# A transformer block in one launch: inputs that arrive channel-major instead of being turned on the chip

## The chip, the cores and the metric

The kernel runs on one core of a Trainium2 chip. The metric is the device time of one execution in microseconds (us). The time before the change is 1368.11 us, the median of 3 runs (1367.45 to 1368.57). The engines are TensorE (PE in the rows; PEld is its weight load), VectorE (DVE), ScalarE (ACT), GpSimd (POOL) and SyncE (SP), whose queue issues all transfers. They run their own instruction lists in order and meet only at semaphores.

## The reference, cut to what matters

One block of a hybrid model, batch 1, 1024 positions, 1024 channels, 4 heads; all in float32. Only what the change touches is shown.

```python
def rmsnorm(x, g):
    xf = x.astype(F32)
    xf = xf * lax.rsqrt(jnp.mean(xf * xf, axis=-1, keepdims=True) + EPS)
    return (xf * g.astype(F32)).astype(x.dtype)

def causal_dwconv(x, w):            # 4 taps, per channel
    y = xp[:, 0:S] * w[0]
    for j in range(1, K):
        y = y + xp[:, j:j + S] * w[j]
    return y

def mlstm_mix(xn, w_in, conv_w, gate_b, norm_g, w_out):
    proj = xn @ w_in
    qk, v, o, g = jnp.split(proj, ...)
    qk = jax.nn.silu(causal_dwconv(qk, conv_w))
    ...                             # chunked scan over 64-step chunks, head norm, output product

memn = rmsnorm(mem, norm_mem)
h = x
h = h + mlstm_mix(rmsnorm(h, norm_mix), ...)
h = h + cross_attn(rmsnorm(h, norm_x), memn, w_q, w_kv, w_o)
h = h + swiglu(rmsnorm(h, norm_ffn), w_gate, w_up, w_down)
return rmsnorm(h, norm_final)
```

## The kernel before, in words

Every product is made of three TensorE products of a high and a low part (`WH`, `WL` of the weights, `XH`, `XL` of the activations); ACT makes the high part, DVE or POOL subtracts it from the full value to get the low one. Activations are kept with channels on the partitions: `xT` is 128 partitions x 8 channel tiles (k) x 1024 positions, worked on in two halves of 512. Weights come in strips of 1 MB into `raw`, in the order of the list `STRIPS`: the first value strip ("v", 0), then for each head its "qk", "v", "o" and the "wo" of the head before, then the memory keys "mk", the last "wo", the memory values "mv", and so on. A strip is worked in groups that go round four PSUM banks; a group can start when the group four before it was taken out of its bank. `PARTS` hangs pieces of other work (the scan of a head, a norm) in front of a group, in the same place on every engine.

**The start.** x arrives with positions on the partitions, in eight tiles of 128 positions x 1024 channels (4 KB a row): four into `xin` (in `VQ`), four into `xlate` (in `XT`). TensorE turns each with eight transposes (`turn_x`); DVE (`tile_of` copies) or ACT (`late_tile`) brings them to `xT`. ACT squares each tile along its row and sums it (`square_x`), POOL makes mean and power -0.5, TensorE spreads the result over the partitions (`spread`), and DVE multiplies x by it and by the gain (`norm`); ACT and DVE split that into `XH` and `XL` (`pieces`). The gain vectors and taps come as rows and are turned once into the columns `vcols`. `first_value(half)` is the value product of 4 position tiles, k by k, 12 products for each k: 4 with `XH` and `GW`, 4 with the weights' low part, 4 with `XL`. The late x tiles 5 to 7 are turned between its first k's. ACT empties the banks of the first half (`evac`) among its pieces of the second: it does the pieces (1, 0) and (1, 1) first, then group 3, whose bank the fourth tile of the second half needs (`bank_at`, `FIRST_OUT`).

**The memory norm.** Between the last "o" strip and the third "wo" strip (head 2) the memory, 256 positions, is normed: ACT squares its two tiles, POOL makes the factor `stat`, DVE multiplies tile, factor and gain (`memnorm`), TensorE turns the two tiles with 16 transposes in front of "wo" group 3 (`memturn`), ACT makes `MH` and DVE `ML` from the banks. The first part of the last head's scan stands in front of "wo" group 6, and waits on TensorE for all of `ML` (`s_ml`), as it uses the same banks.

**The convolution.** For each of the 16 "qk" groups DVE makes four passes over the bank into `acc`: a product with the last tap (L1687), then three multiply-adds (L1690), each linked to the one before; ACT then applies tanh.

Of the kernel before, what the change touches and what calls it, by code (L numbers as in the profile page):

```python
# [10 lines left out]
P = 128  # L11
# [5 lines left out]
def build_block(nc, x, mem, norm_mix, norm_x, norm_ffn, norm_mem, norm_final, a_w_in, a_conv_w, a_gate_b,  # L17
                a_norm, a_w_out, x_w_q, x_w_kv, x_w_o, f_w_gate, f_w_up, f_w_down, out):
# [142 lines left out]
    x_t = x[0].rearrange("(t p) d -> t p d", p=P)  # L161
    mem_t = mem[0].rearrange("(t p) d -> t p d", p=P)
    out_t = out[0].rearrange("(t p) d -> t p d", p=P)
# [8 lines left out]
    with ctx:  # L172
# [25 lines left out]
        NVEC = CONV + TAPS * KT  # L198
# [71 lines left out]
        mxs = mxin  # L270
        gain_mem, mjunk = xin[0], xin[1]
# [8 lines left out]
        vrows = QK[0:NVEC, 0, 0, 0:P]  # L280
# [118 lines left out]
        s_xt = sem("s_xt")  # L399
        s_xh = sem("s_xh")  # L400
        s_xl = sem("s_xl")
        s_vturn = sem("s_vturn")
# [15 lines left out]
        s_xta = sem("s_xta")  # L418
# [12 lines left out]
        s_wt = sem("s_wt")  # L431
        s_wi = sem("s_wi")
# [85 lines left out]
        def tile_of(t, unit):  # L518

            if t < 4 or t == TT - 1:  # L520
                k0, k1, b = 0, KT, 2 * t if t < 4 else 5
            else:
                k0, k1, b = 4 * unit, 4 * unit + 4, 5 + (2 * (t - 4) + unit) % 3
            src = PS[:, b:b + (k1 - k0) // 4, :].rearrange("p a s -> p (a s)").rearrange("p (k s) -> p k s", k=k1 - k0)
            return xT[:, k0:k1, t * P:(t + 1) * P], src

# [5 lines left out]
        def means(c):  # L532

            return 2 * (c + 1) if c < 2 else c + 3
# [55 lines left out]
        def _(sp):  # L590
            def load_strip(n):
# [11 lines left out]
            def load_mu(h):  # L603
# [3 lines left out]
                if h >= 2:  # L607
                    sp.wait_ge(s_wi, TT * (h - 1))
# [11 lines left out]
            for t in range(4):  # L620
                sp.wait_ge(s_xin[t], 16)
                sp.dma_start(xlate[t], x_t[4 + t]).then_inc(s_xin[t], 16)
                if t == 1:
                    sp.dma_start(dst[:, KT // 2:], src[:, KT // 2:]).then_inc(s_wdma, 16)
# [1912 lines left out]
```

## Time and profile before

| | |
|---|---|
| median of 3 runs | 1368.11 us |
| the profiled execution, its own time | 1368.82 us |
| its span in the profile | 1367.1 us |
| PE busy | 1353.3 us (99%) |
| DVE busy | 957.5 us (70%) |
| ACT busy | 511.6 us (37%) |
| POOL busy | 198.6 us (15%) |
| granted TensorE clock, mean | 0.999 |

The span is what the trace covers, the own time is the span with 1.7 us around it. A busy share says how full an engine is on average, not who waits for whom at a place: for that the trace is read by stretches.

### The profile page before, as it was taken

What the parts mean: (1) busy time and instruction counts of PE and PEld (TensorE: products, weight loads), DVE (VectorE), ACT (ScalarE), POOL (GpSimd) and SP (SyncE); (2) the same over time, 40 slices, a digit from 0 to 9 for tenths busy, and PEclk for the clock granted to TensorE, in tenths of its full rate; (3) what the DMA queues carried; (4) which work ended last, traced back from release to release, by engine and by line L of the source; (5) the groups of instructions that cost most, each with busy time, mean ns of one, the idle gap of its engine ahead of it and who ended that gap; (6) DMA issues with size and microseconds to landing.
All of it is one profiled execution on the core that took longest, in us unless ns stands there. A gap on an engine that the chain in (4) does not pass through costs nothing.

```text
span 1367.1 us, 18084 instructions
## 1 busy us (share of the span) xinstructions
PE 1353.3 (99%) x6795; PEld 1148.8 (84%) x6795; DVE 957.5 (70%) x1666; ACT 511.6 (37%) x910; POOL 198.6 (15%) x223
## 2 busy tenths in 40 slices
PE   8999999999999999999999999999999999999998
PEld 8889889889889988888888888888888888888886
DVE  7767467467488875454687966777778778877876
ACT  7323313313335553122345523444344435322224
POOL 3002202202203000000023000000000004544441
PEclk9999999999999999999999999999999999999999
DMA  5211111111223211010032233144434447989903
GB/s 187 62 62 55 55 31 50 60 31 44 97 71 126 85 60 47 17 62 32 31 129 103 78 116 116 55 154 162 169 138 148 154 163 267 329 282 318 341 31 124
DMA packets 110039, 158.56 MB, mean 116 GB/s; under 512 B 6560, under 2 KB 68096, under 8 KB 109952
## 3 DMA queue, kind: packets, MB, share of 16 engines
q1 hardware_dynamic: 109952, 157.39, 33.2%
q8 instruction: 55, 0.90, 0.3%
q14 instruction: 32, 0.26, 0.1%
HBM read 114.89 MB, written 42.48 MB: 115 GB/s over the span
## 4 chain that ended last, share of the span: by engine, by line
PE 90%; DVE 6%; issue 2%; ACT 2%; DMA 1%; POOL 0%; SPq 0%; DVEq 0%; POOLq 0%; ACTq 0%
PE PS L2076 14%; PE PS L2078 14%; PE PS L2077 14%; PE PS L2429 9%; PE PS L2428 9%; PE PS L2430 9%; PE PS L2460 5%; PE PS L2462 5%; PE PS L2461 5%; DVE WL L1757 1%; DVE acc L1690 1%; PE PS L2234 1%; PE PS L2236 1%; PE PS L2238 1%; PE PS L2141 1%
## 5 line engine op out<-in xcount | busy, mean ns | idle before, releaser
L2076 PE MATMUL PS<-XH,WH 128*128 128x512 f32 (+1 forms) x480 | 185.9, 387 | 0.0
L2078 PE MATMUL PS<-XH,WL 128*128 128x512 f32 (+1 forms) x480 | 180.3, 376 | 0.0
L2077 PE MATMUL PS<-XL,WH 128*128 128x512 f32 (+1 forms) x480 | 180.2, 375 | 0.0
L1674 DVE TENSOR_TENSOR xT<-PS,xT 128x512 f32<-128x512 f32 x128 | 87.5, 687 | 44.2 <-PE PS L2078 43.9
L2078 PEld LDWEIGHTS PS<-XH,WL 128*128 128x128 f32 x480 | 90.3, 188 | 16.7
L2076 PEld LDWEIGHTS PS<-XH,WH 128*128 128x128 f32 x480 | 90.4, 188 | 16.0 <-issue 0.4
L2077 PEld LDWEIGHTS PS<-XL,WH 128*128 128x128 f32 x480 | 90.5, 188 | 15.5
L2076 PE MATMUL PS<-YH,WH 128*128 128x512 f32 x256 | 101.4, 396 | 0.0
L2078 PE MATMUL PS<-YH,WL 128*128 128x512 f32 x256 | 99.8, 390 | 0.0
L2077 PE MATMUL PS<-YL,WH 128*128 128x512 f32 x256 | 99.7, 389 | 0.0
L1898 DVE TENSOR_TENSOR xT<-PS,xT 128x512 f32<-128x512 f32 x104 | 70.4, 688 | 39.6 <-PE PS L2462 38.5
L897 POOL TENSOR_TENSOR W2A<-raw,W2A 128x512 fp32r<-128x512 f32 x20 | 28.0, 1400 | 387.7 <-ACT W2A L1279 387.7
L2076 PE MATMUL PS<-WH,XH 128*128 128x256 f32 x256 | 74.2, 290 | 0.2 <-issue 0.2
L2078 PE MATMUL PS<-WH,XL 128*128 128x256 f32 x256 | 72.5, 283 | 0.0
L2077 PE MATMUL PS<-WL,XH 128*128 128x256 f32 x256 | 72.4, 283 | 0.0
L1835 DVE TENSOR_TENSOR U<-PS,U 128x512 f32<-128x512 f32 x50 | 33.5, 688 | 53.8 <-PE PS L2430 53.8
L1757 DVE TENSOR_TENSOR WL<-raw,WH 128x1024 fp32r<-128x1024 f32 x54 | 65.8, 1226 | 2.2 <-ACT WH L930 2.2
L2428 PE MATMUL PS<-XH,WA 128*128 128x512 f32 x160 | 62.2, 389 | 0.0
L2430 PE MATMUL PS<-XH,WA 128*128 128x512 f32 x160 | 62.2, 389 | 0.0
L2428 PE MATMUL PS<-XH,WB 128*128 128x512 f32 x160 | 62.2, 389 | 0.0
L2430 PE MATMUL PS<-XH,WB 128*128 128x512 f32 x160 | 62.2, 389 | 0.0
L1835 DVE TENSOR_TENSOR SG<-PS,SG 128x512 f32<-128x512 f32 x50 | 33.5, 686 | 34.3 <-PE PS L2430 32.7
(408 smaller groups left out, 3489.3 us busy)
## 6 DMA issues: line engine op xcount, KB each, us to landing
forms_hi<-HS SPq DMA_DIRECT2D x56, 256.0 KB, 2.3
raw<-in_f_w_up_dram SPq DMA_DIRECT2D x11, 1024.0 KB, 5.5
rawE<-in_f_w_gate_dram SPq DMA_DIRECT2D x10, 1024.0 KB, 5.7
raw<-in_f_w_down_dram SPq DMA_DIRECT2D x40, 256.0 KB, 4.0
forms_lo<-U SPq DMA_DIRECT2D x32, 256.0 KB, 2.3
XH<-forms_hi SPq DMA_DIRECT2D x16, 512.0 KB, 7.2
raw<-in_a_w_in_dram SPq DMA_DIRECT2D x7, 1024.0 KB, 5.0
XL<-forms_lo SPq DMA_DIRECT2D x12, 512.0 KB, 8.7
```

Of the source, the lines that this page charges most:

```text
L1674: v.tensor_tensor(xt, PS[:, g % NB, :], xt, ALU.add).then_inc(s_fd, 1)
L1757: last = v.tensor_tensor(WL[:, (n + 1) % 2, at], raw_of(n + 1)[:, at], WH[:, (n + 1) % 2, at].bitcast(F32), ALU.subtract)
L1898: v.tensor_tensor(x, bank_of(g, which), x, ALU.add).then_inc(s_ee, 1)
L2076: mm(dst, wh, xh, start=(k == 0), stop=False)
L2077: mm(dst, wh, xl, start=False, stop=False)
L2078: last = mm(dst, wl, xh, start=False, stop=(k == len(tiles) - 1))
L2428: mm(bank, w[:, i, 0, at], xh[:, kk, :], start=start, stop=False, skip_group_check=True)
L2429: mm(bank, w[:, i, 0, at], xl[:, kk, :], start=False, stop=False, skip_group_check=True)
L2430: last = mm(bank, w[:, i, 1, at], xh[:, kk, :], start=False, stop=stop, skip_group_check=True)
L2460: mm(bank, w[:, i, 0, at], xh[:, u, :], start=start, stop=False, skip_group_check=True)
L2461: mm(bank, w[:, i, 0, at], xl[:, u, :], start=False, stop=False, skip_group_check=True)
L2462: last = mm(bank, w[:, i, 1, at], xh[:, u, :], start=False, stop=stop, skip_group_check=True)
```

## The change

x, the memory and all norm gains and taps are also handed over channel-major (`x_turned`, `mem_turned`, `vec_cols`), made before the launch. At the start the first half of x goes straight into `xT` by four transfers of two channel tiles each; ACT squares the even k, DVE the odd k, and TensorE sums each square over the partitions with products against a column of ones (`square_sums`). The second half is loaded twice: by rows, for the squares on ACT, and channel-major for `xT`. All transposes of x, of the vectors and of the memory are gone. For the memory, the turned copy is loaded (`memT`), TensorE turns only the two factor columns, and DVE multiplies, k by k, memory, gain column and spread factor, in the place where `memturn` was; the work of DVE's `memnorm` is dropped. The convolution's first pass is done by ACT. The two semaphores of the scan's exponentials are merged into one. The diff, cut:

```diff
+        sqx = [VQ[:, k // 4, k % 4 * HALF:(k % 4 + 1) * HALF] for k in range(KT)]
+        memT = VQ[:, 0].rearrange("p (k m) -> p k m", k=KT)
+        mjunk = acc[:, :, :].rearrange("p a s -> p (a s)")
...
                 if n == AT["mk", 1]:
-                    sp.wait_ge(s_xs, MT)
-                    sp.wait_ge(s_sq, TT + MT)
+                    sp.wait_ge(s_ml, 2 * MT)
...
-            for t in range(4):
-                sp.dma_start(xin[t], x_t[t]).then_inc(s_xin[t], 16)
-            for v, at, n in ((norm_x, NORM_X, KT), (norm_ffn, NORM_F, KT), (a_norm, A_NORM, KT), (norm_mix, NORM_M, KT)):
-                sp.dma_start(vrows[at:at + n, :], v[0].rearrange("(k p) -> k p", p=P)).then_inc(s_vec, 16)
+            first = slice(0, HALF)
+            for i in range(4):
+                at = slice(2 * i, 2 * i + 2)
+                sp.dma_start(xT[:, at, first], x_k[:, at, first]).then_inc(s_xin[i], 16)
             dst, src = strip_src("v", 0)[0]
             sp.dma_start(dst[:, 0:KT // 2], src[:, 0:KT // 2]).then_inc(s_w0, 16)
             sp.dma_start(wg_raw, cols(a_w_in, G0, 2 * H)).then_inc(s_wg, 16)
+            sp.dma_start(vcols[:, :], vec_cols).then_inc(s_vec, 16)
+            sp.dma_start(dst[:, KT // 2:], src[:, KT // 2:]).then_inc(s_wdma, 16)
             for t in range(4):
                 sp.wait_ge(s_xin[t], 16)
                 sp.dma_start(xlate[t], x_t[4 + t]).then_inc(s_xin[t], 16)
+            for i in range(2):
+                at = slice(4 * i, 4 * i + 4)
+                sp.dma_start(xT[:, at, HALF:], x_k[:, at, HALF:]).then_inc(s_xlt, 16)
...
                     tap = CONV + KT * (TAPS - 1) + (r % 2) * H + h
+                    act.wait_ge(s_mm, g + 1)
+                    if c >= 2:
+                        act.wait_ge(s_qk, c - 1)
+                    sc.activation(acc[:, r % 2, :], bank, ACT.Copy, scale=vcols[:, tap:tap + 1]).then_inc(s_tap, 1)
                     act.wait_ge(s_conv, c + 1)
...
+            def square_chunk(i):
+                act.wait_ge(s_xin[i], 16)
+                sc.activation(sqx[2 * i], xT[:, 2 * i, 0:HALF], ACT.Square).then_inc(s_sq, 1)
...
             for k in range(KT):
                 pieces(0, (k,))
-                if k == 1:
-                    late_tile(4)
-                if k == 2:
-                    late_tile(5)
-                if k == 3:
-                    square_x(4)
-                    late_tile(6)
-                if k == 4:
-                    square_x(5)
-                if k == 5:
-                    square_x(6)
-                    square_x(7)
+                if 2 <= k <= 5:
+                    square_x(2 + k)
...
+            def memturn(a, b):
+                dve.wait_ge(s_gain, 16)
+                dve.wait_ge(s_turn, MT)
+                for k in range(KT):
+                    last = v.scalar_tensor_tensor(out=memT[:, k, :], in0=memT[:, k, :],
+                                                  scalar=vcols[:, NORM_MEM + k:NORM_MEM + k + 1], in1=X0[:, 0:M],
+                                                  op0=ALU.mult, op1=ALU.mult)
+                    if k % 4 == 3:
+                        last.then_inc(s_xs, 1)
+                for q in range(4):
+                    dve.wait_ge(s_mh, q + 1)
+                    at = slice(2 * q, 2 * q + 2)
+                    v.tensor_tensor(ML[:, at, :], memT[:, at, :], MH[:, at, :].bitcast(F32), ALU.subtract).then_inc(s_ml, 1)
...
                     if c == 1:
-                        dve.wait_ge(s_xta, 2 * NT - 2)
+                        dve.wait_ge(s_xlt, 32)
...
-                    if (c, k) in ((0, KT - 1), (1, KT - 1), (3, LATE[1]), (5, KT - 1)) and waiting:
+                    if (c, k) in ((1, KT - 1), (3, LATE[1]), (5, KT - 1)) and waiting:
                         make_lo()
...
-                    link(v.tensor_scalar(a, bank, tap(TAPS - 1), None, ALU.mult))
...
+            def keep_busy(count):
+                for _ in range(count):
+                    mm(PS[:, 7, 0:P], ones[:, :], ones[:, :], start=True, stop=True)
+
+            def square_sums(k):
+                pe.wait_ge((s_sq, s_sqv)[k % 2], k // 2 + 1)
+                for t in range(NT):
+                    last = mm(PS[:, t, 0:1], sqx[k][:, t * P:(t + 1) * P], one, start=(k == 0), stop=(k == KT - 1),
+                              skip_group_check=True)
+                if k == KT - 1:
+                    last.then_inc(s_xsum, 1)
...
-            for t in range(4):
-                turn_x(t)
+            for k in range(KT):
+                square_sums(k)
+            keep_busy(5)
             spread(0, 0)
+            keep_busy(5)
```

**TensorE at the start**, its first rows before (`ones` are products that only fill time, `VQ` holds the first four x tiles, `XT` the late ones, `small` the norm factor, `GW` and `WL` the first value weights):

```order
1 L2353 MATMUL PS<-ones 128x128 x7
2 L2347 MATMUL PS<-ident,VQ 128x128 x32
3 L2360 MATMUL PS<-ident,QK 128x64
4 L2363 MATMUL PS<-ident 128x128 x4
5 L2278 MATMUL PS<-ident,small 128x128 x4
6 L2347 MATMUL PS<-ident,XT_90 128x128 x8
7 L2163 MATMUL PS<-GW,XH 128x272 x4
8 L2168 MATMUL PS<-WL,XH 128x256 x4
9 L2172 MATMUL PS<-GW,XL 128x264 x4
10 L2347 MATMUL PS<-ident,XT_90 128x128 x8
```

and now (`VQ` holds the squares, `small` in row 2 is the column of ones):

```order
1 L2307 MATMUL PS<-ones 128x128 x9
2 L2313 MATMUL PS<-small,VQ 128x1 x32
3 L2307 MATMUL PS<-ones 128x128 x5
4 L2248 MATMUL PS<-ident,small 128x128 x4
5 L2307 MATMUL PS<-ones 128x128 x5
6 L2140 MATMUL PS<-GW,XH 128x272 x4
7 L2145 MATMUL PS<-WL,XH 128x256 x4
8 L2149 MATMUL PS<-GW,XL 128x264 x4
9 L2140 MATMUL PS<-GW,XH 128x272 x4
```

The 32 transposes have become 32 sums with one column each, 12 filling products are more (9, 5 and 5 for 7), and no transposes stand between the k's of the value product.

**VectorE at the end of the first half's norm**, before (a row with `s_rt` is the first norm of the second half; `XL` rows are low parts):

```order
16 L1587 SCALAR_TENSOR_TENSOR acc<-xT,vcols,PS 128x512 [waits s_xl]
17 L1733 COPY xT<-PS 128x8x128 [waits s_turn]
18 L1571 TENSOR_TENSOR XL<-SG,XH 128x512 [waits s_xh]
19 L1587 SCALAR_TENSOR_TENSOR acc<-xT,vcols,PS 128x512 [waits s_xl]
20 L1571 TENSOR_TENSOR XL<-acc,XH 128x512 [waits s_xh] x2
21 L1587 SCALAR_TENSOR_TENSOR SG<-xT,vcols,PS 128x512 [waits s_xl,s_xta,s_rt]
22 L1587 SCALAR_TENSOR_TENSOR SG<-xT,vcols,PS 128x512 [waits s_xl]
23 L1571 TENSOR_TENSOR XL<-SG,XH 128x512 [waits s_xh]
```

and now:

```order
19 L1576 SCALAR_TENSOR_TENSOR acc<-xT,vcols,PS 128x512 [waits s_xl]
20 L1560 TENSOR_TENSOR XL<-SG,XH 128x512 [waits s_xh]
21 L1576 SCALAR_TENSOR_TENSOR acc<-xT,vcols,PS 128x512 [waits s_xl]
22 L1560 TENSOR_TENSOR XL<-acc,XH 128x512 [waits s_xh]
23 L1576 SCALAR_TENSOR_TENSOR SG<-xT,vcols,PS 128x512 [waits s_xl,s_xlt,s_rt]
24 L1560 TENSOR_TENSOR XL<-acc,XH 128x512 [waits s_xh]
25 L1576 SCALAR_TENSOR_TENSOR SG<-xT,vcols,PS 128x512 [waits s_xl]
```

The copy of a turned tile is gone, and the low part of k = 7 of the first half (the second of row 20 before, row 24 now) has moved behind the first norm of the second half, which waits for its spread factor (`s_rt`) and its loads (`s_xlt`).

**VectorE at the memory norm**, around the third "wo" strip, before (`xT<-PS,xT` adds a "wo" group to the residual, `WL<-raw,WH` is the low part of the next weights):

```order
488 L1538 SCALAR_TENSOR_TENSOR QK<-QK,small,VQ 128x1024 [waits s_rs,s_gain]
489 L1538 SCALAR_TENSOR_TENSOR QK<-QK,small,VQ 128x1024 [waits s_rs]
490 L1532 TENSOR_SCALAR SG<-SG 128x512 [waits s_fa] x4
491 L1674 TENSOR_TENSOR xT<-PS,xT 128x512 [waits s_mm]
492 L1757 TENSOR_TENSOR WL<-raw,WH 128x1024 [waits s_whi]
493 L1674 TENSOR_TENSOR xT<-PS,xT 128x512 [waits s_mm]
494 L1757 TENSOR_TENSOR WL<-raw,WH 128x1024 [waits s_whi]
495 L1674 TENSOR_TENSOR xT<-PS,xT 128x512 [waits s_mm]
496 L1546 TENSOR_TENSOR XL<-PS,XH 128x4x128 [waits s_mh] x4
497 L1674 TENSOR_TENSOR xT<-PS,xT 128x512 [waits s_mm] x3
```

and now:

```order
475 L1521 TENSOR_SCALAR SG<-SG 128x512 [waits s_fa] x4
476 L1663 TENSOR_TENSOR xT<-PS,xT 128x512 [waits s_mm]
477 L1736 TENSOR_TENSOR WL<-raw,WH 128x1024 [waits s_whi]
478 L1663 TENSOR_TENSOR xT<-PS,xT 128x512 [waits s_mm]
479 L1736 TENSOR_TENSOR WL<-raw,WH 128x1024 [waits s_whi]
480 L1663 TENSOR_TENSOR xT<-PS,xT 128x512 [waits s_mm]
481 L1528 SCALAR_TENSOR_TENSOR VQ<-VQ,vcols,PS 128x256 [waits s_turn,s_gain]
482 L1528 SCALAR_TENSOR_TENSOR VQ<-VQ,vcols,PS 128x256 x7
483 L1536 TENSOR_TENSOR XL<-VQ,XH 128x512 [waits s_mh] x4
484 L1663 TENSOR_TENSOR xT<-PS,xT 128x512 [waits s_mm] x3
```

Two multiplications of 1024 elements ahead of the strip have become eight of 256 inside it, directly in front of the four low parts that complete `s_ml`.

## Rows read from the trace of the kernel before

**Rows 1.** Busy time by stretch: us, PE, PEld, DVE, ACT, POOL, clock, DMA.

```profile
42.00:130.00 88.00, 87.74 (x448) 74.11 (x447) 61.72 (x159) 28.17 (x59) 6.17 (x10) 1.00 0.19 58
```

**Rows 2.** PE's waits over the span: us in total, times, longest.

```profile
PE PS L2201 <- DVE hs L1505: 0.8, 3, 0.3
```

**Rows 3.** The start in order of time: start us, us, what.

```profile
4.44 1.06 ACT L935 ACTIVATE QK<-VQ 128x1024 f32<-128x1024 f32 x1 [2.36 <-DMA VQ<-in_x_dram]
9.36 1.09 PE L2347 MATMUL PS<-ident,VQ 128*128 128x128 f32 x8 [0.18 <-DMA VQ<-in_x_dram]
11.44 0.65 PE L2278 MATMUL PS<-ident,small 128*128 128x128 f32 x4 [0.20 <-POOL small L850]
12.13 1.41 DVE L1587 SCALAR_TENSOR_TENSOR SG<-xT,vcols,PS 128x512 f32<-128x512 f32 x2
13.69 0.74 PE L2163 MATMUL PS<-GW,XH 128*128 128x272 f32 x4
```

**Rows 4.** One line's instructions: count, ns min/median/max, first and last start.

```profile
L2353 PE MATMUL PS<-ones x14: 421/421/579, 1.2 to 4.1; 128*128 128x128 f32 x14
```

**Rows 5.** The column sums of the next norm, and POOL's power, in order of time.

```profile
450.01 1.05 PE L2262 MATMUL PS<-small,QK 128*128 128x1 f32 x8 [0.26 <-DVE QK L1556]
451.10 0.16 DVE L1563 COPY small<-PS 128x4 f32<-128x4 f32 x1 [0.55 <-PE PS L2262]
451.63 1.02 POOL L860 TENSOR_TENSOR small<-small 128x4 f32<-128x4 f32 x1
```

**Rows 6.** The first value product in order of time.

```profile
23.12 1.06 ACT L935 ACTIVATE QK<-XT 128x1024 f32<-128x1024 f32 x1
29.41 0.53 PE L2163 MATMUL PS<-GW,XH 128*128 128x272 f32 x3
30.12 0.39 PE L2163 MATMUL PS<-GW,XH 128*128 128x272 f32 x1 [0.18 <-ACT zg L1108]
```

**Rows 7.** The chain that ended last, inside the second half.

```profile
32.94 0.50 PE PS L2163 x4
...
34.41 0.51 PE PS L2163 x4
```

**Rows 8.** DMA activity at the start, columns as in rows 1.

```profile
16.00:17.00 1.00, 1.00 (x11) 1.00 (x10) 1.00 (x3) 0.70 (x2) 0.90 (x1) 1.00 0.26 85
```

**Rows 9.** The memory norm in order of time.

```profile
374.67 1.91 ACT L930 ACTIVATE WH<-raw 128x2048 fp32r<-128x2048 f32 x1
...
376.95 1.21 DVE L1757 TENSOR_TENSOR WL<-raw,WH 128x1024 fp32r<-128x1024 f32 x1
378.07 1.91 PE L2247 MATMUL PS<-ident,QK 128*128 128x128 f32 x16
...
380.42 2.47 DVE L1546 TENSOR_TENSOR XL<-PS,XH 128x512 fp32r<-128x512 f32 x4
...
383.91 0.27 PE L2218 MATMUL PS<-ident,QK 128*128 128x128 f32 x1
```

**Rows 10.** TensorE in the same stretch: where "wo" group 3 begins.

```profile
379.73 0.48 PE L2076 MATMUL PS<-YH,WH 128*128 128x512 f32 x1
```

**Rows 11.** Two DVE instructions in a row: 256 elements from PSUM, then another.

```profile
389.52 0.48 DVE L1501 TENSOR_SCALAR hs<-PS,small 128x256 f32<-128x256 f32 x1
389.92 0.68 DVE L1674 TENSOR_TENSOR xT<-PS,xT 128x512 f32<-128x512 f32 x1
```

**Rows 12.** The same multiplication form as the new one, 257 elements, by line.

```profile
L1491 DVE SCALAR_TENSOR_TENSOR Cst<-Cst,decay,PS x24: 474/482/485, 105.1 to 423.2; 128x257 f32<-128x257 f32 x24
```

**Rows 13.** After the last matmul, columns as in rows 1; the clock stands third from the end.

```profile
1360.00:1361.00 1.00, 0.29 (x2) 0.00 (x0) 0.67 (x2) 0.00 (x0) 0.53 (x1) 1.00 0.67 274
...
1363.00:1364.00 1.00, 0.00 (x0) 0.00 (x0) 0.86 (x2) 0.00 (x0) 0.10 (x1) 0.96 0.95 393
1364.00:1365.00 1.00, 0.00 (x0) 0.00 (x0) 0.55 (x1) 0.00 (x0) 0.00 (x0) 0.50 0.57 227
```

**Rows 14.** The convolution's first and later passes, by line.

```profile
L1687 DVE TENSOR_SCALAR acc<-PS,vcols x16: 740/745/751, 47.2 to 321.6; 128x512 f32<-128x512 f32 x16
```

More of the change, by code:

```diff
@@ L993, in memturn @@
                 act.wait_ge(s_mm, used(AT["o", H - 1]))
[L994 to L999 removed]
+                for q in range(4):
+                    act.wait_ge(s_xs, q // 2 + 1)
+                    at = slice(2 * q, 2 * q + 2)
+                    sc.activation(MH[:, at, :], memT[:, at, :], ACT.Copy).then_inc(s_mh, 1)
             def square(n, r):
@@ L1145, in split_first @@
                               ACT.Copy).then_inc(s_w0h, 1)
-            for t in range(4):
-                square_x(t)
+            for i in range(4):
+                square_chunk(i)
             split_first()
@@ L1711, in evac @@
                     add_residual(g, r)
-            for t in range(4):
-                dve.wait_ge(s_turn, t + 1)
-                dst, src = tile_of(t, 0)
-                v.tensor_copy(dst, src).then_inc(s_xt, 1)
-            dve.wait_ge(s_vturn, 1)
-            link(v.tensor_copy(vcols[:, :], PS[:, 0, 0:NVEC]))
+            for i in range(4):
+                dve.wait_ge(s_xin[i], 16)
+                full = xT[:, 2 * i + 1, 0:HALF]
+                v.tensor_tensor(sqx[2 * i + 1], full, full, ALU.mult).then_inc(s_sqv, 1)
+            dve.wait_ge(s_xsum, 1)
+            sums = PS[:, 0:NT, 0:1].rearrange("p t a -> p (t a)")
+            v.tensor_scalar(nmean[:, 0, :], sums, 1.0 / D, EPS, ALU.mult, ALU.add).then_inc(s_nm, 1)
+            dve.wait_ge(s_vec, 16)
             dve.wait_ge(s_wgs, 1)
@@ L1726, in _ @@
                             ALU.subtract).then_inc(s_wlo, 1)
-            norm(0, 5)
-            make_lo()
-            waiting.append((0, 5))
-            norm(0, 6)
-            dve.wait_ge(s_turn, TT)
-            dst, src = tile_of(TT - 1, None)
-            v.tensor_copy(dst, src).then_inc(s_xt, 1)
-            make_lo()
-            waiting.append((0, 6))
-            pieces(0, (7,))
+            pieces(0, range(5, KT))
             pieces(1, range(KT))
@@ L2241, in memturn @@
             def memturn(a, b):
+                pe.wait_ge(s_rs, MT)
+                pe.wait_ge(s_yf, TT * (H - 1))
                 for t in range(MT):
-                    pe.wait_ge(s_xs, t + 1)
-                    if t == 0:
-                        pe.wait_ge(s_yf, TT * (H - 1))
-                    for q in range(KT):
-                        last = nc.tensor.transpose(PS[:, NB + 2 * t + q // 4, (q % 4) * P:(q % 4 + 1) * P],
-                                                   mxs[:, t, q * P:(q + 1) * P], ident[:, :])
-                    last.then_inc(s_turn, 1)
+                    nc.tensor.transpose(X0[:, t * P:(t + 1) * P], stat[:, t, 2:3].to_broadcast([P, P]),
+                                        ident[:, :]).then_inc(s_turn, 1)
             def sumsq(which, half):
@@ L2351, in _ @@
+            def square_sums(k):
[5 more added lines that the diff above has]
+                    last.then_inc(s_xsum, 1)
             pe.wait_ge(s_const, 2)
-            for _ in range(7):
-                mm(PS[:, 7, 0:P], ones[:, :], ones[:, :], start=True, stop=True)
+            keep_busy(9)
```

145 lines of the change are left out of this document (46 added, 99 removed).

## The prediction, made before the changed kernel ran

> **What bounds the kernel now.** I read the busy time by stretch first: from 42 us on TensorE is busy 87.74 of 88 us [rows 1], and the later stretches look alike. Then its waits: the longest behind the start is 0.8 us in three pieces, for the scan's `hs` [rows 2]. So a microsecond taken from VectorE or ScalarE in the middle is worth nothing, and one taken from TensorE is worth one, as long as it doesn't come to wait. Only two places matter: the start, where TensorE waits for x, the norm and the splits, and the memory norm, where 16 transposes are in its list. I read both in order of time.
>
> **The start, up to the first norm.** Before: the first x tile is there at 4.44, the last is turned from 9.36, the spread starts at 11.44, the first norm at 12.13, the first value product at 13.69, 1.56 behind it [rows 3]. Now the same 2 MB come first, so I let them land at the same times (4.4 to 9.3). The nine filling products are 18 entries in the trace where seven were 14; those began between 1.2 and 4.1, 0.223 apart [rows 4], so 18 reach to about 5.1 (a little less if the later ones run faster). The first square (half of the 1.06 us of a 1024-wide one, so about 0.6 [rows 3]) is ready by then. Then come 32 column sums. The nearest row is exact in form: four of them are 8 entries and take 1.05 us, the last being visible 0.15 behind its place, so 0.11 each and 0.89 for four [rows 5]. Eight k's make 7.1 us: from 5.1 to 12.3. They are spaced so that TensorE, not the landing at 9.3, sets the end (the last two k's alone would need 1.8 from about 10.0). Then, as after the later sums: 0.1 to VectorE, 0.2 there, 0.1 to POOL, 1.02 for a power of four columns [rows 5], 0.06 to TensorE and 0.65 for the spread [rows 3], 0.04 to VectorE: first norm at 14.5. The five filling products in between (10 entries at 0.11) lie inside POOL's 1.3 us, the other five inside the 1.56 us from norm to product. **So the first norm comes 2.4 us later.** Bounds: if a column sum cost only its one column, the end would be set by the last landing, 9.3 + 0.65 + some 0.2, plus 2.2 of chain, 12.3: +0.2. If all ran at the spacing of the first fillers, 0.223, the sums would take 14.3 us: +9.6.
>
> The Trainium skill, page "TensorE: Matmul & The Clock Gate", section "Back-to-back issue gap", gives about 60 cycles for a matmul of 1 to 64 columns, some 25 ns. By that rule 64 entries would be an estimated 1.6 us, the sums would hide behind the landing, and the whole sum below would be 2.2 us less. The row is of the same instruction with its weight load and decides.
>
> **From the first norm to the second half.** Before, the second half's first product starts at 29.41 [rows 6], 17.28 behind the first norm. In that time TensorE also turned three late tiles, VectorE copied one, ScalarE copied three. Without them I lay the lists out anew, t from the first norm: a norm on VectorE 0.67 (two in 1.41 [rows 3]), a low part 0.60 (four in 2.47 [rows 9]), a weights' low part 1.2 [rows 9], on ScalarE a high part 0.6 and a late square 1.06 [rows 6], on TensorE 1.47 a k (32.94 to 34.41 [rows 7]). k = 0 starts at 1.56; k = 4 needs the second half of the weights' low part, behind the norm of k = 4 on VectorE: 7.7 instead of 7.4; the low part of k = 4 is then 0.3 late; k = 5 at 9.5, k = 6 at 10.95. At 12.4 stands the second spread (0.45); its power is ready at about 11.5. The low part of k = 7 now stands behind the first norm of the second half, which waits for that spread: norm 13.05 to 13.7, low part to 14.4, wanted at 13.85: 0.6 of stall. The second half starts at 14.95: **2.3 us gained**. One wait grows: its fourth tile needs the bank that ScalarE empties behind pieces (1, 0) and (1, 1). The norm of (1, 1) now ends at 15.1, ScalarE's piece at 15.75, the emptying at 16.4, against 15.35 wanted (three products of 0.13 [rows 7] behind the start): 1.05 of stall, where before it was 0.33 (30.12 against 29.41 and the same three [rows 6]): **0.7 lost**. The transfers: before, all was landed just after 16 us [rows 8]; x's second copy adds 2.1 MB, and at the pace of x's tiles, three of 0.52 MB from 4.44 to 9.3 [rows 3], that is 6.5 us, to 23; the norm of the second half wants it at 27.5. Hidden by 4.5 us; without the cover it would cost what it is late. Start in all: 2.4 - 2.3 + 0.7 = **+0.8 us**.
>
> **The convolution.** 16 passes of 0.745 [rows 14] leave VectorE, 12 us, and some 16 of 0.6 come to ScalarE, which waits there for the passes anyway. TensorE is four banks ahead; it gets at most the 0.8 us of rows 2 from it. I take -0.2, bounds -0.8 and, if ScalarE comes late with a first pass because of the scan in its list, +0.5.
>
> **The memory norm.** Before: the 16 transposes start at 378.07 [rows 9], "wo" group 3 at 379.73 [rows 10], the scan's first part behind group 5 at 383.91 [rows 9]: 1.66 for the transposes, 4.18 for three groups. VectorE is done with `ML` at 382.89 (380.42 + 2.47 [rows 9]), 1.0 before it is wanted. Now the two transposes leave group 3 at 378.3 and the scan's part comes up at 382.45. But VectorE: the strip's weights are ready at 376.6 (374.67 + 1.91 [rows 9]), its two low parts and two residual adds take 3.5 as before (376.95 to 380.42 [rows 9]), from 376.65 since `memnorm` is out of the way: 380.1. Then eight multiplications of 256 elements with a PSUM operand: of that form one lasts 0.48 [rows 12], and 0.40 passes from one such to the next instruction [rows 11]: 3.2. Then four low parts, 2.5 with the last one's end: 385.8. ScalarE's four high parts keep ahead (its last at 384.6). So `s_ml` is complete at 385.8 instead of 382.9, TensorE stands for 3.4 us and the scan's part starts at 385.85: **+1.9 us** against 383.91. Bounds: no wait left, -1.45 (14 transposes); multiplications at their full 0.48, +2.6. Nothing later gives it back, since TensorE is the bound; VectorE has evacuations of groups 3 to 5 behind it (to 387.8), and the bank of group 3 is free at 386.5, before group 7 wants it. The transfer of the next key weights now waits for `s_ml` as well, 10 us later than before; it lands by 392 and nobody reads it before the memory keys, past 400.
>
> **The sum.** 0.8 - 0.2 + 1.9 = +2.5 us. The profiled execution took 1368.82 (span 1367.1 and 1.7 around it), so it would take 1371.3; it lies 0.7 over the median of the runs shown, so the median goes from 1368.11 to **1370.6**, 0.18% slower. 0.2% (2.7 us) is about what a measurement of this kernel can tell from no change, so this lies just inside.
>
> **The rivals.**
> *The clock falls during the sums, slower.* For 7 us TensorE would do nothing but load weights and send one column. The first fillers took 421 ns each, with the column of the granted clock at 1.00 [rows 4]; a product of the same size lasts 270 later [rows 9], so these ran at the lower level of 1.2 GHz, and behind some 3.3 us of fillers back to back it was over. After the last matmul the granted clock falls to 0.50, 3.6 us later (0.96 in the mean of 1363 to 1364) [rows 13]. If it falls during the sums, say for their second half, those run at 0.22 apart (+3.9), the next fillers outlast POOL (+0.9), the spread and the first products are slow (+1.7): 6.5 more, 1377. No row shows TensorE at such work for longer than 1 us, so little speaks for or against. The same could strike the 3.4 us stall at the memory norm, which is just short of 3.6. Chance 0.2. The skill, in the same page's section "What's actually happening", says that the slow state is the default and activity releases it, which bears on this rival; by it the time would be the same 1377.
> *VectorE keeps up at the memory norm.* If the chain from 380.1 ends before 382.45, the transposes are a pure gain: 0.8 - 0.2 - 1.45, 1367.3. It needs multiplications and low parts in 2.3 us where rows give 5.7; only if TensorE comes there late for another reason. Chance 0.12.
> *The sums hide, not slower.* If a column sum costs what its column does, the first norm is at 12.3, and the whole -2.2 + 2.5: 1368.4. It decides from 0.05 us an entry down, where the landing at 9.3 takes over. Chance 0.12; together with the one before, 1365.1, another 0.08: the only clear gain.
> The forecast itself 0.48, spread from 1369 to 1372.
>
> **The numbers.** Faster by over 0.2% is below 1365.4: the double case and a little, 0.12. Slower by over 0.2% is above 1370.8: the clock's 0.2 and 0.46 of the forecast's 0.48, 0.42. Within: 0.46. For the range I leave out the double gain below and the dear end of the clock's case above: 1366.5 to 1376.5; the forecast's own is 1369 to 1372.
>
> **What will show it.** The first norm at 14.5, the 64 sum entries from 5.1 to 12.3, 0.11 apart; the second half's first product at 29.4 or 29.5 with a wait for ScalarE's `zg` of 1 us behind it; all later work shifted by 0.8. At the memory norm a wait of TensorE for `XL` from VectorE of 3.4 us, the largest behind the start, in front of the scan's transposes. It is wrong if the sums' spacing is not 0.11, if the granted clock or the durations show the lower level beyond 5 us, or if TensorE doesn't wait for `XL`.

## The result, and the profile after

The changed kernel took **1377.56 us** in the median of six runs (1376.48 to 1378.87), the kernel before 1367.87 (1367.32 to 1368.57, six runs beside them): ratio 1.007, 95% interval 1.006 to 1.008. It is 9.7 us slower, where 2.5 were forecast, and outside the range. The profiled execution spans 1375.1 us, 8.0 more than before.

The changed kernel in order of time, first the start, then the memory norm (start us, us, what):

```profile
4.86 0.63 ACT L1131 ACTIVATE VQ<-xT 128x512 f32<-128x512 f32 x1 [2.79 <-DMA xT<-in_x_turned_dram]
5.63 11.38 PE L2313 MATMUL PS<-small,VQ 128*128 128x1 f32 x64 [0.43 <-ACT VQ L1131]
9.15 0.63 ACT L1131 ACTIVATE VQ<-xT 128x512 f32<-128x512 f32 x1 [0.69 <-DMA xT<-in_x_turned_dram]
16.88 2.48 PE L2307 MATMUL PS<-ones 128*128 128x128 f32 x10
17.30 1.04 POOL L842 TENSOR_TENSOR small<-small 128x4 f32<-128x4 f32 x1 [14.44 <-DVE small L1705]
19.15 1.06 PE L2248 MATMUL PS<-ident,small 128*128 128x128 f32 x4
20.25 1.41 DVE L1576 SCALAR_TENSOR_TENSOR SG<-xT,vcols,PS 128x512 f32<-128x512 f32 x2 [2.88 <-PE PS L2248]
21.96 0.75 PE L2140 MATMUL PS<-GW,XH 128*128 128x272 f32 x4
...
384.56 3.21 DVE L1528 SCALAR_TENSOR_TENSOR VQ<-VQ,vcols,PS 128x256 f32<-128x256 f32 x8
387.69 2.49 DVE L1536 TENSOR_TENSOR XL<-VQ,XH 128x512 fp32r<-128x512 f32 x4
390.32 0.30 PE L2195 MATMUL PS<-ident,QK 128*128 128x128 f32 x1 [3.32 <-DVE XL L1536]
395.02 0.27 PE L2195 MATMUL PS<-ident,QK 128*128 128x128 f32 x1
```

These answer to [rows 3] and [rows 9]. The transfers land nearly as forecast (4.86 to 9.15, against 4.4 to 9.3). The 64 entries of the column sums last 11.38 us in place of 7.1, although TensorE does nothing else; the first norm stands at 20.25 (forecast 14.5, before 12.13) and the first value product at 21.96. The same kernel by stretch (us, PE, PEld, DVE, ACT, POOL, granted clock, DMA), which answers to [rows 1] and [rows 13]:

```profile
6.00:8.00 2.00, 2.00 (x20) 2.00 (x20) 0.86 (x2) 0.80 (x2) 0.00 (x0) 1.00 1.02 362
8.00:10.00 2.00, 2.00 (x12) 2.00 (x13) 1.22 (x2) 1.09 (x2) 0.00 (x0) 0.57 1.12 348
10.00:20.00 10.00, 10.00 (x47) 10.00 (x48) 0.31 (x2) 1.20 (x2) 2.70 (x3) 0.50 1.06 403
20.00:22.00 2.00, 2.00 (x12) 2.00 (x11) 1.71 (x3) 0.94 (x2) 1.77 (x2) 0.52 0.93 353
22.00:24.00 2.00, 2.00 (x18) 2.00 (x18) 2.00 (x4) 1.24 (x3) 0.00 (x0) 1.00 0.06 18
42.00:130.00 88.00, 88.00 (x456) 74.92 (x455) 57.46 (x151) 32.65 (x66) 3.89 (x7) 1.00 0.20 61
386.00:390.00 4.00, 1.00 (x5) 0.50 (x3) 4.00 (x9) 2.88 (x6) 0.00 (x0) 1.00 0.00 0
390.00:391.00 1.00, 0.68 (x4) 0.71 (x5) 1.00 (x3) 0.34 (x2) 0.00 (x0) 0.78 0.00 0
391.00:394.00 3.00, 3.00 (x8) 2.33 (x8) 2.08 (x6) 0.61 (x3) 0.00 (x0) 0.50 0.80 249
394.00:400.00 6.00, 6.00 (x29) 4.99 (x29) 4.20 (x12) 1.46 (x5) 0.73 (x2) 1.00 0.64 225
```

The granted clock, third from the end, falls to 0.50 during the sums (near 8.3 us, by the mean of 0.57 over 8 to 10) and is back when the value products run; twenty entries show in the two microseconds before the fall, 47 in the ten behind it. It falls once more behind the stall at the memory norm, for some 3.4 us. That stall heads TensorE's waits (us in total, times, longest); the wait of [rows 2] for `hs` is gone:

```profile
PE PS L2195 <- DVE XL L1536: 3.3, 1, 3.3
PE PS L2307 <- POOL small L781: 1.2, 1, 1.2
PE PS L2178 <- DVE yf L1505: 0.6, 2, 0.4
```

**Where the 8.0 us lie.** I cut the two traces at four places that both have. The first 512-wide product starts at 47.47 instead of 41.58: start +5.9. From there to the transposes of the memory norm 335.05 us instead of 336.49: middle -1.4. From those to the scan's first part 7.80 instead of 5.84: +2.0. From there to its second part 4.70 instead of 3.12: +1.6. From there to the end nothing. The places that no row above shows, before and then changed:

```profile
41.58 0.39 PE L2076 MATMUL PS<-XH,WH 128*128 128x512 f32 x1
...
387.03 0.27 PE L2218 MATMUL PS<-ident,QK 128*128 128x128 f32 x1
```

```profile
47.47 0.39 PE L2055 MATMUL PS<-XH,WH 128*128 128x512 f32 x1
...
382.52 0.38 PE L2222 MATMUL PS<-ident,small 128*128 128x128 f32 x2
```

### The profile page after: what moved, and what is told of

Its sections match the earlier page's. It is cut to its first block, busy times and chain, and to the rows that moved or that the text cites. A ratio compares the mean times of both kernels' runs of the same rounds, so it can differ in the third digit from the quotient of the medians.

```text
span 1375.1 us, 18072 instructions
## 1 busy us (share of the span) xinstructions
PE 1360.0 (99%) x6800; PEld 1157.5 (84%) x6800; DVE 943.0 (69%) x1655; ACT 517.1 (38%) x916; POOL 195.3 (14%) x220
## 4 chain that ended last, share of the span: by engine, by line
PE 66%; DVE 3%; issue 1%; ACT 1%; POOL 0%; DVEq 0%; POOLq 0%; ACTq 0%
PE PS L2389 9%; PE PS L2388 9%; PE PS L2387 9%; PE PS L2055 7%; PE PS L2057 7%; PE PS L2056 7%; PE PS L2419 5%; PE PS L2420 5%; PE PS L2421 5%; DVE WL L1736 1%; PE PS L2120 1%; PE PS L2122 1%; PE PS L2121 1%; PE PS L2448 1%; PE PS L2279 0%
## 5 line engine op out<-in xcount | busy, mean ns | idle before, releaser
L2055 PEld LDWEIGHTS PS<-XH,WH 128*128 128x128 f32 x480 | 90.4, 188 | 16.1 <-issue 0.4
L2057 PEld LDWEIGHTS PS<-YH,WL 128*128 128x128 f32 x256 | 48.4, 189 | 10.3
```

The lines of the kernel that those rows point to most:

```text
L2055: mm(dst, wh, xh, start=(k == 0), stop=False)
L2057: last = mm(dst, wl, xh, start=False, stop=(k == len(tiles) - 1))
```

## The experiments

Every kernel is compared with the changed one (1377.56) unless said otherwise. Two marks from each trace help, since they separate the start from the rest: when the first 512-wide product starts, and how long the span lasts from there. The kernel before ran beside every group of kernels again, with medians of 1367.64 to 1368.50, so a difference of less than 0.9 us between kernels of different groups is not shown.

| kernel | median us | first 512-wide product | from there to the end |
|---|---|---|---|
| before | 1367.87 | 41.58 | 1325.5 |
| changed | 1377.56 | 47.47 | 1327.6 |
| e2: fillers between the sums | 1381.98 | 52.43 | 1327.6 |
| s1: sums 128 columns wide | 1372.90 | 42.30 | 1329.7 |
| s2: half the sums, more fillers | 1376.07 | 46.34 | 1325.3 |
| m1: memory path of before | 1374.65 | 47.46 | 1323.4 |
| e3: stall filled | 1375.08 | 47.48 | 1325.5 |
| e4: memory products earlier | 1376.04 | 49.95 | 1325.1 |
| e5: s1, memory path spread | 1367.91 | 42.55 | 1323.8 |
| f1: s1, half the sums, m1 | 1367.29 | 42.83 | 1323.6 |
| b1: before, convolution on ScalarE | 1366.69 | 41.29 | 1324.1 |
| b2: b1, memory path spread | 1365.90 | 41.46 | 1322.6 |

**e2, fillers between the column sums.**

```diff
             for k in range(KT):
                 square_sums(k)
+                if k < KT - 1:
+                    keep_busy(2)
```

> The changed kernel with two filling products (ones by ones, 128 columns) behind each of the first seven sets of column sums. Theory: TensorE's clock falls to its lower level because of what it does during the sums, and that is what makes them take 11.4 instead of 7.1 us. Then the granted clock stays at 1.00 from 5 to 22 us, the entries of the sums stay 0.11 apart, sums and fillers end at 5.6 + 7.1 + 3.1 = 15.8 instead of 17.0, the fillers and the spread behind them are 1.7 us quicker, and the first norm starts near 18.0 instead of 20.25: about 2.3 us less than the changed kernel, 1375. Rival: the column sums are slow for another cause (their weights are read while transfers fill the same memory) and the clock's column only shows idle: then their entries stay about 0.18 apart and the fillers come on top, first norm near 23, 1380.

1381.98 (1381.75 to 1384.9, four runs), ratio to the kernel before 1.0105 (1.0092 to 1.0119). In order of time:

```profile
7.16 0.95 PE L2313 MATMUL PS<-small,VQ 128*128 128x1 f32 x8
...
8.50 0.95 PE L2313 MATMUL PS<-small,VQ 128*128 128x1 f32 x8
9.31 1.11 PE L2307 MATMUL PS<-ones 128*128 128x128 f32 x4
10.21 1.71 PE L2313 MATMUL PS<-small,VQ 128*128 128x1 f32 x8
```

Eight entries show 0.95 us before the fall and 1.71 behind it, in one trace and with the same operands, so it is the clock that slows them, not the reads of the squares or the transfers beside them. The fillers did not keep the clock up, so the theory's 1375 failed. By stretch:

```profile
8.00:10.00 2.00, 2.00 (x17) 2.00 (x18) 1.23 (x2) 1.11 (x2) 0.00 (x0) 0.85 1.10 355
```

A mean of 0.85 between the two levels puts the fall near 9.4 us. Without fillers it was near 8.3 in the changed kernel, and near 7.9 and 8.7 in e3 and m1, which have the same sums. So it came somewhat later, and most of the fillers only added work at the low level.

**s1, the same sums with 128 columns.**

```diff
-                    last = mm(PS[:, t, 0:1], sqx[k][:, t * P:(t + 1) * P], one, ...
+                    last = mm(PS[:, t, 0:P], sqx[k][:, t * P:(t + 1) * P], ones[:, :], ...
```

> The changed kernel, but each of the 64 column sums multiplies its tile of squares with a 128x128 tile of ones in place of one column of ones (the sum then stands 128 times in a bank, and the first of them is read). Theory A: it is the narrow products, in which the engine streams one column for a load of 128, that let the granted clock fall from 1.00 to 0.50 at 8.3 us; with 128 columns, as in the fillers, it stays at 1.00, the 64 sums end near 14 us in place of 17.0 (0.13 us for each, as the fillers take), the first norm stands near 16, and the time is some 5 us under the changed kernel's 1377.6: about 1372.5. Theory B: the clock falls in this stretch whatever the width of the products: then the sums end at 17 us or later (128 columns at the low clock), and the time is 1377.6 or more.

1372.90 (1372.65 to 1373.82, four runs), 4.7 under the changed kernel; ratio to the kernel before 1.0038 (1.0023 to 1.0053). In order of time:

```profile
5.49 7.38 PE L2313 MATMUL PS<-ones,VQ 128*128 128x128 f32 x64
14.93 1.41 DVE L1576 SCALAR_TENSOR_TENSOR SG<-xT,vcols,PS 128x512 f32<-128x512 f32 x2 [1.71 <-PE PS L2248]
16.48 0.74 PE L2140 MATMUL PS<-GW,XH 128*128 128x272 f32 x4 [0.47 <-ACT XH L1025]
```

and by stretch:

```profile
8.00:10.00 2.00, 2.00 (x20) 2.00 (x19) 1.12 (x2) 1.00 (x2) 0.00 (x0) 1.00 1.14 337
10.00:12.00 2.00, 2.00 (x20) 2.00 (x19) 0.00 (x0) 1.04 (x2) 0.00 (x0) 1.00 1.13 388
```

Each product now streams 128 times as many columns, and the 64 entries take 7.38 us instead of 11.38, 0.115 each, about what the narrow ones take at the high level. The clock stays at 1.00. Theory A holds: with one column the clock fell in this stretch, with 128 it stayed, and nothing else was changed. The first norm is at 14.93 and the first 512-wide product 0.7 us behind the kernel before, where the prediction had 14.5 and 0.8.

**s2, half as many narrow sums, more fillers.** VectorE adds the two squares of a chunk, and four calls of `keep_busy` stand between sets.

```diff
             for i in range(4):
...
+                dve.wait_ge(s_sq, i + 1)
+                v.tensor_tensor(sqx[2 * i], sqx[2 * i], sqx[2 * i + 1], ALU.add).then_inc(s_sqv, 1)
...
-            for k in range(KT):
+            for k in range(0, KT, 2):
                 square_sums(k)
+                if k < KT - 2:
+                    keep_busy(4)
```

> The changed kernel, but VectorE adds the two squares of a chunk, so that 32 column sums are left, with four fillers (eight entries) of the 128x128 ones product ahead of each of the last three sets of eight. VectorE is done with the last pair near 10.6 us (landing at 9.15, 0.69 for the square, 0.69 for the sum). Theory A (the clock is lost by too long a run of narrow products): the clock holds, the last sum ends near 11.6, the first norm stands near 14, and the time is some 6 us under the changed kernel: about 1371.5. Theory B (the clock falls in spite of the fillers, as it did in the run with two fillers behind each set): the last set takes 1.7 us at the low clock, ends near 12.5, the first norm stands near 15.5 and the low clock lasts into the first products: about 1373.5.

1376.07 (1373.72 to 1378.61, four runs). Theory B: the clock still fell, at about 9 us, with as many wide fillers as narrow sums in the list, and the last set ended at 16.1, not at 12.5. By stretch:

```profile
8.00:10.00 2.00, 2.00 (x16) 2.00 (x15) 1.92 (x4) 1.18 (x2) 0.00 (x0) 0.72 1.11 353
```

Half as many narrow products are no cure, and the time is 2.6 us over what theory B gave.

**m1, the memory path of before in the changed kernel.** The gain as a row, `memnorm` on VectorE, 16 transposes, high and low parts out of the banks.

> The changed kernel with the memory path of the kernel before: memory row-major from memory, the gain as a row, both normalized on VectorE ahead, 16 transposes at the third group of the output projection, its high and low parts read from the banks. Theory: this path's share of the loss is the wait of 3.3 us on TensorE (1.96 us more than the path before cost at that place) and the low clock behind it (1.6 us): the time falls by about 3.6 us against the changed kernel, to 1374.0, and the granted clock between 374 and 400 us is 1.00. Rival: the path is masked by work behind it, and the time stays within 1 us of 1377.6; what is lost then is the start's alone.

1374.65 (1372.65 to 1375.69, four runs): 2.9 less; in the traces 4.2 less behind the start. The stall is gone and the clock is 1.00 from 22.4 us to 1360. The sign and the place are right. The median mixes two kinds of runs, which the last section tells apart: the profiled one took 1372.65, the other three 1374.53 to 1375.69. Against the changed kernel's runs of the same kind that is 4.3 and 3.9 less, so the 3.6 of the theory is borne out.

**e3, the stall filled.** 14 calls of the 128x128 ones product (28 entries) stand in front of the scan's wait for `s_ml`.

> The changed kernel with 14 filling products on TensorE in front of the scan's first part of the last head, where it stands 3.3 us for the memory's low parts. The wait stays (28 entries of 0.11 are 3.1 us). Theory: the stall costs twice, 1.96 us by itself against before and 1.6 us more because the granted clock falls at its end and stays low for 3.3 us. Then the clock stays at 1.00 there, the distance from the factor's two transposes to the scan's part stays 7.8 us, and the distance from that part to the next one falls from 4.7 to 3.1: 1.6 us less than the changed kernel, about 1376.0. Rival: the slower products behind the stall come from banks and VectorE being late, not from the clock: then that distance stays at 4.7 and the time at 1377.6.

1375.08 (1374.14 to 1377.24, four runs), 2.5 less; in the traces 2.1. In order of time:

```profile
386.85 3.29 PE L2194 MATMUL PS<-ones 128*128 128x128 f32 x28
390.24 0.33 PE L2197 MATMUL PS<-ident,QK 128*128 128x128 f32 x1
...
393.37 0.27 PE L2197 MATMUL PS<-ident,QK 128*128 128x128 f32 x1
```

The scan's first part comes no earlier (390.24 against 390.32), the second 1.65 us earlier, 3.13 behind the first as in the kernel before. So the wait costs 2.0 and the clock behind it 1.6, in this execution.

**e4, products at the first group of the output projection.** TensorE spreads the factor and VectorE multiplies at group 0 instead of 3; the low parts come at groups 3, 4, 9 and 10; the scan waits for the products alone.

> The changed kernel with the memory norm taken apart: the two factor transposes and VectorE's eight multiplications in front of group 0 of the third output strip instead of group 3, the four low parts one each in front of groups 3, 4, 9 and 10, and the scan's first part waits for the multiplications (which read its bank) and no more for the low parts. Theory: the whole loss at the memory norm is VectorE's 5.7 us between group 2 and the scan. Then TensorE's wait for XL is gone, the scan's part starts 1.45 us nearer to the strip's start than before the change, and the time is 1.96 + 1.6 + 1.45 = 5.0 us under the changed kernel: 1372.6. Rival: the eight small multiplications only move the wait: VectorE is late with the residual adds of groups 0 to 2, and TensorE waits for banks there, 1 to 3 us: 1374 to 1376.

1376.04 (1375.13 to 1377.16, four runs): 1.5 less. TensorE's waits:

```profile
PE PS L2059 <- DVE xT L1667: 2.1, 1, 2.1
PE PS L2199 <- DVE wT L1466: 0.6, 1, 0.6
```

The rival holds: the wait for `XL` has become one for a bank whose residual add is late. VectorE stood idle for 2.4 us in front of it, for the weights that ScalarE converts:

```profile
386.41 1.90 ACT L930 ACTIVATE WH<-raw 128x2048 fp32r<-128x2048 f32 x1
...
388.35 1.23 DVE L1740 TENSOR_TENSOR WL<-raw,WH 128x1024 fp32r<-128x1024 f32 x1 [2.42 <-ACT WH L930]
```

ScalarE's high parts stood ahead of that conversion and waited for VectorE's products. So VectorE was not full, the order was wrong. Behind the start this trace is 2.5 us shorter than that of the changed kernel; its start is 2.5 us longer, which the last section takes up.

**e5, wide sums and the memory path in a better order.**

```diff
+    part("wo", H - 2, 0, ("memturn", 0, None))
+    part("wo", H - 2, 1, ("memhi", 0, None))
+    for q in range(4):
+        part("wo", H - 2, (4, 5, 9, 10)[q], ("memlow", q, None))
...
                     for t in range(MT):
                         sp.dma_start(mxin[:, t, :], mem_t[t]).then_inc(s_min[t], 16)
+                    sp.dma_start(memT, mem_k).then_inc(s_gain, 16)
```

> The kernel with wide column sums (1372.9), with the memory path moved again: memory row-major is fetched ahead of memory channel-major, TensorE spreads the factor at the first group of the output projection, VectorE multiplies there, ScalarE makes the high parts at the second group, behind the conversion of the next weights, and VectorE makes the four low parts at groups 4, 5, 9 and 10; the scan waits for the products alone. In the run with the products at the first group VectorE stood idle for 2.4 us since the conversion of the weights waited behind the high parts, and this is mended. Theory: the two waits of that run (2.1 and 0.6 us) shrink to 1 us or less in all, the clock stays at 1.00 there, and the time is 1369.4. Rival: VectorE has no room for 5.7 us of memory work in these 22 us whatever the order, the wait returns at the banks (2 us or more), and the time is 1371 or more.

1367.91 (1366.9 to 1368.84, ten runs); ratio to the kernel before 0.9996 (0.9987 to 1.0005). One wait is left there,

```profile
PE PS L2200 <- DVE wT L1467: 0.5, 1, 0.5
```

and the clock stays up. The gain over s1 is 5.0, more than the 3.5 expected; in its trace s1 had paid 2.7 us for the clock behind its stall. Two edits thus undo the whole loss of 9.7 us, with the gain of the convolution (b1) still in the time.

**f1, wide sums of pairs, memory path of before.**

> The changed kernel with three edits: VectorE adds the two squares of a chunk, the 32 column sums left multiply with 128 columns of ones, with two fillers (four entries) between sets; and the memory path is that of the kernel before. Theory: the clock stays at 1.00 through the start, the last set of sums begins when the last pair is added (near 10.7 us) and ends near 11.6, the first norm stands near 13.8 and the first value product near 15.4 (14.93 and 16.48 with 64 wide sums), so that the time is 1372.9 less 1.1 less 3.0 for the memory path: 1368.8, no better than the kernel before with the convolution on ScalarE alone (1366.7). Rival: the start's earlier norm is eaten by a later wait of the second half's row-major tiles, and the time stays at 1369.9 or above.

1367.29 (1366.31 to 1369.42, 11 runs); ratio 0.9995 (0.9986 to 1.0004). The time is lower than expected and the reason given was wrong: the first norm comes at 15.46, not at 13.8 and later than in s1. TensorE waits 1.0 us for the first pair, and the entries behind the wait run at the low level until about 10 us (eight of them take 2.05, later 1.06), although the clock's column says 1.00; the last set ends at 13.4. The wait is not shown to be the cause: s2 waited 0.93 at the same place, and its first eight sums behind it took 1.02. Behind the start it equals e5 (1323.6 and 1323.8): e5 is 1.3 ahead at the scan's second part and loses 1.5 from there to the end. That loss is not shown to come from the memory path, since b2 has the same path and does not have it.

**b1, the convolution alone, in the kernel before.** The first pass of the convolution goes to ScalarE as in the diff; nothing else changes.

> The kernel before with one part of the change: the convolution's first pass on ScalarE (and the merged semaphore). Between the first strip and the memory norm the changed kernel lost less than before: from the first 512-wide product to the memory's transposes it is 1.3 us shorter. Theory: that is this part, by TensorE's waits for the scan's hs and their stalled weight loads (7 of them, now 1): 1366.6, 1.3 us under before. Rival: my forecast of 0.2 us was right and the 1.3 come from the later start of everything there: 1367.7.

1366.69 (1366.4 to 1367.48, 11 runs); ratio 0.9989 (0.998 to 0.9998). That is 1.8 us under the 1368.50 of the kernel before that ran beside it and 1.2 under the 1367.87 above, so more than the rival's 0.2 either way. TensorE's wait for `hs` between 42 and 374 us [rows 2] goes from 0.8 to:

```profile
PE PS L2236 <- DVE hs L1506: 0.3, 1, 0.3
```

In the traces 0.9 us go between the first 512-wide product and the memory norm, 0.3 at the start, which this edit does not touch, and 0.5 behind.

**b2, the best parts together.** The kernel before with its own start, b1, and the memory path of e5 (the gain as eight more rows of the vectors that it transposes).

> The kernel before with its own start (tokens row-major, transposed on the chip), the convolution's first pass on ScalarE, and memory channel-major in the spread order (factor and products at the first group of the output projection, high parts at the second, low parts at groups 4, 5, 9 and 10; the gain of memory as eight more rows of the vectors that are transposed at the start). Theory: up to the scan's second part the spread memory path took 343.1 us from the first 512-wide product on, against 344.5 with the memory path before; its 16 transposes are gone and nothing waits in their place but 0.5 us. So the time is 1366.7 less 1.4: 1365.3, the lowest of all. Rival: what is saved there is lost behind the final projections' residual adds, where the spread version showed 0.6 us of waits that the kernel before had only 0.2 us of (from the last transposition of the scan to the end 961.8 us against 960.8): then 1366.3 or the 1366.7 of the convolution alone.

**1365.90** (1365.47 to 1367.27, 11 runs), ratio to the kernel before 0.9984 (0.9975 to 0.9993): 2.2 us faster than the kernel before and 11.7 than the changed one. It is 0.8 under b1, between the two figures expected; b1 ran in another group, the two intervals overlap, and so this last step is not clear of noise. In the traces it is 1.5 behind the start.

## Why the prediction was wrong

**The step that failed** is the price of a column sum: "0.11 each and 0.89 for four ... Eight k's make 7.1 us: from 5.1 to 12.3". The row behind it was of eight entries in the midst of wide products [rows 5], at the clock that those had. At that level the price is right (in e2 twelve entries, eight sums and four fillers, take 1.34 us from 7.16 to 8.50, and s1's 64 take 7.38). But here the clock falls at 8.3, and from there on an entry takes 0.21: 11.4 in all, then POOL's chain, the fillers and the spread at the low clock, and the first norm comes 8.1 later instead of 2.4. That the clock was the cause and not the sums' number is shown by s1, which changes the width alone and puts the first norm at 14.93, and by e2, where one trace has both prices.

The prediction had this case as a rival, "the clock falls during the sums", at 6.5 us more and 1377, with a chance of 0.2. The mechanism and the place were right, the chance too low and the size somewhat too large (s1 gives back 5.2 at the first 512-wide product). That its 1377 met the measured 1377.56 is partly luck: the start cost 1.3 less and the convolution gave 1.2 more than in it, and against this stood 1.6 for the clock behind the stall, which it did not price, and the runs' spread. What should have raised the chance stood in its own rows: the level had risen behind fillers [rows 4] and fallen with no product [rows 13], so it followed what TensorE did, and no row had it under narrow products alone for more than 1 us.

The Trainium skill's section "What's actually happening" (page "TensorE: Matmul & The Clock Gate"), cited there, says that the slow state is the default and activity releases it. The first fillers, at 421 ns, agree [rows 4]. The fall here came while TensorE was busy for 2.00 of 2.00 us with one-column products, and in s1, with 128 columns, it did not come; the sentence does not say which of the two to expect. The Trainium skill's section "Back-to-back issue gap", on the same page, gives its 25 ns for a matmul by itself; of a stream in which each matmul has its weight load it says that both set the pace. That agrees with the 0.11 us an entry here, and made the 25 ns the wrong figure for these sums; the prediction rightly went by the row.

**Landings, norm to second half.** The landings were right. From the first norm to the second half's first product it took 14.69 us (14.95 forecast), the wait for `zg` is 0.5 instead of 1.05, and the one of 0.5 for `XL` (L2149) was there as forecast (0.6). From the first norm to the first 512-wide product that makes 2.2 us less than before, where 1.6 less were forecast (-2.3 and +0.7). In s1, with the clock kept, it is 2.1 less and the first norm 2.8 later (2.4 forecast): its start is 0.7 later, 0.8 forecast, close because two misses cancel.

**The convolution.** Right sign, mis-sized: -0.2 forecast, -1.2 to -1.8 measured alone (b1, medians), -1.4 in the middle of the changed kernel. All of the wait in [rows 2] went, which is 0.8; where the rest comes from is not shown. The lower bound of -0.8 was too near.

**The memory norm.** Right to 0.1: `XL` complete at 390.2 (385.8 forecast, and everything before it is 4.45 later), a stall of 3.32 (3.4 forecast), the scan's part 1.96 later (1.9). A second step failed here: the sum put the clock behind the stall at nothing, and in this execution it cost 1.6; the rival named it in one sentence and gave it no price.

**The sum.** 5.89 - 1.44 + 1.96 + 1.58 = 7.99, against 0.8 - 0.2 + 1.9 + 0.

The medians lie 1.7 us further apart than the two spans (9.7 against 8.0), since the profiled execution of before was 0.95 over its median and that of the changed kernel 0.63 under. Half of the changed kernel's six runs lie near 1376.8 and half near 1378.5; the last section shows a mechanism that fits.

## What to carry to other kernels

A price taken from a row holds for the clock of that row: before many small products are put where nothing wide runs beside them, ask what keeps the clock up there. Products with one column, each with its own weight load, could here be made 128 wide at no cost (7.38 us for 64 entries), and that was the cheapest repair. When work is moved to channel-major form, count what leaves the bounding engine against what lands on the engine that it waits for, and look at the order on the third engine (here ScalarE's conversion) before calling an engine full.

## What the runs showed of the hardware that was not expected

**A busy TensorE can lose its clock.** With single-column products it was busy for the whole of 6 to 10 us, and the granted clock went from 1.00 to 0.50.

**The low level from the first entry on, unseen in the clock's column.** In e4 the same 64 sums began at the same time and took 2.4 us more. In order of time, and by stretch:

```profile
5.65 13.79 PE L2317 MATMUL PS<-small,VQ 128*128 128x1 f32 x64 [0.26 <-ACT VQ L1133]
```

```profile
6.00:8.00 2.00, 2.00 (x11) 2.00 (x11) 0.99 (x2) 0.93 (x2) 0.00 (x0) 1.00 1.02 367
10.00:20.00 10.00, 10.00 (x48) 10.00 (x48) 0.31 (x2) 1.20 (x2) 0.28 (x1) 1.00 1.06 405
```

Eleven entries in these 2 us, where the changed kernel had twenty, is the low level's pace, and the column says 1.00 all the way. So at the start the column can't be trusted and the durations have to be read, as with the first fillers [rows 4].

This fits the two kinds of runs of the changed kernel. A run in which the clock never rises before the sums would be about 2 us longer and would show a higher mean clock, since its column misses the fall. The mean clock of every run bears this out: in each of the six kernels with narrow sums (changed, e2, e3, e4, m1, s2) the runs with a mean of 0.997 or more are slower than all the others, 10 runs of 26. In e4 the two at 0.999 took 1376.87 and 1377.16, the two at 0.994 1375.13 and 1375.2; in the changed kernel the two at 0.997 took 1378.40 and 1378.87, three at 0.992 and 0.993 took 1376.48 to 1376.93, and one at 0.991 took 1378.19, which this does not explain. Only e4 has a trace of the longer kind, so for the other kernels it is argued and not shown.

**The same stall, three prices.** TensorE stood for 3.32 us at the memory norm in the changed kernel, in s1 and in s2, with the same work around it. The scan's second part followed the first after 4.70, 5.79 and 3.10 us: the clock was at the low level for 3.4 us, for 6.8, and not at all. By stretch, s2 across its stall, and s1 behind its own:

```profile
385.00:388.00 3.00, 0.87 (x4) 0.38 (x2) 3.00 (x8) 2.48 (x5) 0.00 (x0) 1.00 0.00 0
388.00:391.00 3.00, 1.81 (x10) 1.59 (x11) 3.00 (x6) 1.35 (x5) 0.00 (x0) 1.00 0.19 34
```

```profile
381.00:385.00 4.00, 0.83 (x4) 0.37 (x2) 4.00 (x10) 2.89 (x6) 0.00 (x0) 0.89 0.00 0
386.00:390.00 4.00, 4.00 (x11) 3.13 (x10) 2.18 (x6) 0.59 (x3) 0.00 (x0) 0.50 0.95 292
```

A stall of this length had no fixed price here: 2.0 us for the wait and 0, 1.6 or 2.7 behind it, in one trace each.
